# Stationary operands of the expert products widened from 96 to 128 columns

## The reference

```
def clamped_swiglu(h):
    glu, lin = h[..., ::2], h[..., 1::2]
    glu = jnp.minimum(glu, SWIGLU_LIMIT)
    lin = jnp.clip(lin, -SWIGLU_LIMIT, SWIGLU_LIMIT)
    return glu * jax.nn.sigmoid(SWIGLU_ALPHA * glu) * (lin + 1.0)

def expert_block(args):
    tok, gate, e = args
    hid = xt[tok] @ w1[e] + b1[e]          # 1024 -> 2048
    out = clamped_swiglu(hid) @ w2[e] + b2[e]   # 1024 -> 1024
    return out * gate[:, None].astype(out.dtype)
```

## Time and profile before

| | |
|---|---|
| executions, median of three | 1666.47 us (1656.95 to 1667.12) |
| span of the profiled execution | 1658.8 us |
| TensorE busy | 1594.8 us, 96% |
| VectorE busy | 1331.5 us, 80% |
| ScalarE busy | 1027.0 us, 62% |
| GpSimd busy | 609.0 us, 37% |
| HBM read | 443.67 MB |

### The profile page before, as it was taken

How to read it: one execution, slowest core, us unless ns; L and a number is a source line. 1 busy time by engine, 2 the same in 40 slices (tenths; PEclk the granted TensorE clock), 3 DMA queues, 4 the chain that set the end, 5 groups by cost and what they waited for, 6 DMA issues and landing times.

```text
span 1658.8 us, 23226 instructions
## 1 busy us (share of the span) xinstructions
PE 1594.8 (96%) x7860; PEld 1161.0 (70%) x7860; DVE 1331.5 (80%) x1172; ACT 1027.0 (62%) x890; POOL 609.0 (37%) x398
## 2 busy tenths in 40 slices
PE   6999989999998999999999999999999999999993
PEld 5787867897566667777777777777777777777772
DVE  4489755543487999899899899899899899999892
ACT  4534335321366777777777777777777777777772
POOL 5643611331342213434333434333434333434320
PEclk9999989999998999999999999999999999999996
DMA  5322100201569999999999999999999999999984
GB/s 178 123 76 77 15 13 1 103 2 53 191 229 310 370 392 380 368 374 384 377 375 380 372 375 379 381 373 380 369 380 378 379 371 377 378 373 383 381 332 135
DMA packets 146542, 467.08 MB, mean 282 GB/s; under 512 B 21014, under 2 KB 35004, under 8 KB 146428
## 3 DMA queue, kind: packets, MB, share of 16 engines
q1 hardware_dynamic: 136684, 437.36, 70.0%
q0 software_dynamic: 9664, 28.53, 7.3%
q10 hardware_dynamic: 144, 0.52, 0.1%
HBM read 443.67 MB, written 22.71 MB: 281 GB/s over the span
## 4 chain that ended last, share of the span: by engine, by line
PE 86%; DVE 5%; DMA 4%; issue 2%; POOL 1%; ACT 1%; SPq 1%; POOLq 0%; DVEq 0%; ACTq 0%
PE banks L1675 21%; PE banks L1677 20%; PE banks L1676 20%; PE banks L1337 2%; PE banks L1620 2%; PE banks L1338 2%; PE banks L1339 2%; PE banks L1684 2%; PE banks L1526 1%; PE banks L1670 1%; PE banks L1516 1%; PE banks L1403 1%; PE banks L1704 1%; PE banks L1428 1%; DMA x_sum<-xs 1%
## 5 line engine op out<-in xcount | busy, mean ns | idle before, releaser
L2017 DVE TENSOR_TENSOR lo<-slots,hi 128x2048 fp32r<-128x2048 f32 x384 | 862.9, 2287 | 55.0 <-PE banks L1677 48.6
L1126 ACT CAST hi<-slots 128x2048 fp32r<-128x2048 f32 x384 | 733.7, 1911 | 243.7 <-PE banks L1677 124.8
L1675 PE MATMUL banks<-lo,x_hi 128*96 128x512 f32 x1024 | 408.1, 399 | 0.0
L1677 PE MATMUL banks<-hi,x_lo 128*96 128x512 f32 x1024 | 403.4, 394 | 0.0
L1676 PE MATMUL banks<-hi,x_hi 128*96 128x512 f32 x1024 | 402.3, 393 | 0.0
L914 POOL DMA_INDIRECT x_sum<-hT,idy x32 | 91.6, 2862 | 464.5 <-ACT hT L1215 450.0
L939 POOL COPY idx_all<-ovf_pair 96x2 int32 x28 | 162.5, 5803 | 157.4 <-DMA ovf_pair<-slot_tokens,ovf_col 157.4
L1677 PEld LDWEIGHTS banks<-hi,x_lo 128*96 128x96 f32 x1024 | 165.8, 162 | 72.3
L1676 PEld LDWEIGHTS banks<-hi,x_hi 128*96 128x96 f32 x1024 | 166.4, 162 | 67.3
L1675 PEld LDWEIGHTS banks<-lo,x_hi 128*96 128x96 f32 x1024 | 165.9, 162 | 66.6
L1675 PE MATMUL banks<-lo,a_hi 128*96 128x512 f32 x512 | 202.8, 396 | 5.7 <-DVE a_lo L2205 4.1
(11 more groups left out here) (370 smaller groups left out, 1946.9 us busy)
## 6 DMA issues: line engine op xcount, KB each, us to landing
slots<-in_expert_w_dram SPq DMA_DIRECT2D x384, 1024.0 KB, 10.7
slots<-in_w_in_dram SPq DMA_DIRECT2D x13, 1024.0 KB, 5.1
xs<-in_x_dram SPq DMA_DIRECT2D x8, 512.0 KB, 5.9
slots<-in_w_out_dram SPq DMA_DIRECT2D x2, 2048.0 KB, 7.9
x_sum<-xs SPq DMA_DIRECT2D x4, 512.0 KB, 9.4
h_rows<-slots SPq DMA_DIRECT2D x4, 512.0 KB, 3.6
xs<-x_sum SPq DMA_DIRECT2D x4, 512.0 KB, 6.8
x_sum<-xs POOLq DMA_DIRECT2D x3, 512.0 KB, 10.1
```

The lines of the kernel that those rows point to most:

```text
L1126: nc.scalar.copy(w_hi[n % HI][:, :, :], raw[r]).then_inc(hi_ready, 1)
L1675: nc.tensor.matmul(out, x_h, w_l, start=first, stop=False)
L1677: return nc.tensor.matmul(out, x_l, w_h, start=False, stop=last)
L2017: tensor_tensor(w_lo[n % LO][:, :, :], raw[n % RAW], w_hi[n % HI][:, :, :], ALU.subtract).then_inc(lo_ready, 1)
```

## The change

The stationary operands of the expert and bias matmuls become 128 columns wide. The data do not: of x and a the 96 slots of a slice are followed, within the 128 columns, by the first 32 words of what lies behind them in memory, which is the next slice, and behind the last slice 32 words that are cleared once (OVER). x_hi and x_lo become two halves of one tensor, so that behind the last slice of x_hi comes x_lo. The results of those further columns land in partitions 96 to 127 of the PSUM banks, and no one reads them. The selection matrices get 128 columns of the same expert, as two tensors in different regions; the second is therefore filled later, when its region is free.

```
-        x_hi, x_lo = (rounded(f"x_{nm}", "BK", BW, o, [P, KT, NS]) for nm, o in (("hi", 3 * CW), ("lo", 3 * CW + KT * NS)))
-        a_hi = rounded("a_hi", "BK", BW, 3072, [P, FT, NS])
-        sel = rounded("sel", "BK", BW, 3072 + FT * NS, [P, 2, NS])
-        a_lo = rounded("a_lo", "hT", BW, 3 * D, [P, FT, NS])
+        OVER = P - NS
+        x_parts = rounded("x_parts", "BK", BW, 3 * CW, [P, 2 * KT * NS + OVER])
+        a_parts = [rounded("a_hi", "BK", BW, 3 * CW + 2 * KT * NS + OVER, [P, FT * NS + OVER]),
+                   rounded("a_lo", "hT", BW, 3 * D, [P, FT * NS + OVER])]
+        sel = [rounded("sel0", "BK", BW, 3 * CW + 2 * KT * NS + FT * NS + 2 * OVER, [P, P]),
+               rounded("sel1", "hT", BW, 3 * D + FT * NS + OVER, [P, P])]
+        x_hi, x_lo = (x_parts[:, o:o + KT * NS].rearrange("p (k s) -> p k s", s=NS) for o in (0, KT * NS))
+        a_hi, a_lo = (t[:, 0:FT * NS].rearrange("p (k s) -> p k s", s=NS) for t in a_parts)
+
+        def x_columns(part, k):
+            return x_parts[:, (part * KT + k) * NS:(part * KT + k) * NS + P]
+
+        def a_columns(part, f):
+            return a_parts[part][:, f * NS:f * NS + P]
...
-                        nc.tensor.matmul(bank[2 + c][0:NS, :], sel[:, q, :], b1r[:, c * CW:(c + 1) * CW], start=True, stop=False)
+                        nc.tensor.matmul(bank[2 + c], sel[q][:, :], b1r[:, c * CW:(c + 1) * CW], start=True, stop=False)
...
-                        ins = three_products(bank[2 + 2 * half + c][0:NS, :], x_hi[:, k, :], x_lo[:, k, :],
+                        ins = three_products(bank[2 + 2 * half + c], x_columns(0, k), x_columns(1, k),
...
-                        ins = three_products(bank[6 + h][0:NS, :], a_hi[:, f, :], a_lo[:, f, :],
+                        ins = three_products(bank[6 + h], a_columns(0, f), a_columns(1, f),
...
-                nc.vector.tensor_copy(sel[:, q, :].unsqueeze(2), expert_row[:, bass.ds(e, 1)].unsqueeze(1).to_broadcast([P, NS, 1]))\
+                nc.vector.tensor_copy(sel[q][:, :].unsqueeze(2), expert_row[:, bass.ds(e, 1)].unsqueeze(1).to_broadcast([P, P, 1]))\
...
                     if st == ("o", 1, 1):
                         dve.wait_ge(g2_in, 16)
+                        step(nc.vector.memset(x_parts[:, 2 * KT * NS:].bitcast(f32), 0.0))
+                        step(nc.vector.memset(a_parts[0][:, FT * NS:].bitcast(f32), 0.0))
                         set_expert(0, 0)
-                        set_expert(1, 1)
...
             x_low(0, True)
+            step(nc.vector.memset(a_parts[1][:, FT * NS:].bitcast(f32), 0.0))
+            set_expert(1, 1)
             for k in range(1, W1U):
```

## The result

The change made the kernel a little slower. Twenty runs of each kernel give a median of 1665.45 us after (1663.98 to 1673.06) against 1661.76 before (1655.61 to 1667.12), a ratio of 1.0035 with an interval of 1.0023 to 1.0047. That is within 1%, but clearly no gain, and the forecast was 1652 (on the scale of the first three runs of before; 0.9913 of 1661.76 would be 1647). The profiled execution of after has a span of 1663.4 us, against 1658.8.

The account below looks back on a forecast made before the run. TensorE's own matmul stream, 231 ns a step, was taken to pace the expert loop; 29 blocks x 0.48 us (13.9), plus 0.5 and 0.1, made about 14.5 us saved: 1652 on the median's scale, range 1643 to 1668.

Parts of the forecast that it names:

- item 1: Expert-block weight and bias matmuls: 146 steps each 4.2 ns less (230.9 to 226.7), 0.61 us gained per block.
- the paragraph on width: Compared input projection (128 columns, 226.7 ns) with expert loop (4.3 ns more) and put the difference down to width.
- (a): Last w2 product, 96 columns with DMA nearly idle, still takes 230.9 ns a step, so traffic is not what costs.
- (b): Input projection's short product with 8 stationary columns takes 231.1 ns a step, so narrow is slow there too.
- The first rival: Width isn't it: expert-loop step stays at 230.9 ns, 1.6 us lost, 1668 on the median's scale; chance 0.23.
- Items 2 and 3: After each of two transpose groups per block: nine unsettled steps give back 0.08 us, the uncovered first load 0.05.
- Loads: Stationary loads take 191 ns at 128 columns instead of 162 at 96, hidden behind the running matmul.
- Items 5 to 8: Extra PSUM rows free; selection row at most 0.07 us, covered; clears and moved row 0 to 0.4 us once; other engines unchanged.
- The supply: Expert-loop weight transfers must rise from 377 to 382 GB/s; 391 was seen, so no bound, but a close one.
- the milder form of that rival: Expert-loop transfers limited to 380 GB/s: only 8 us gained, 1658; chance 0.11 for supply limiting part or all.
- The rival "slower": Wider expert-stream matmuls never settle and take 235 ns a step, costing 19 us, 1685; chance 0.06.
- The fast load: 128-column loads fall from 191 to about 96 ns, 5.5 us more gained, 1646; chance 0.02.

Follow-up runs that it names:

- pad128: The changed kernel with every 128-column stationary slice in its own 512 bytes, all starting at byte 128; 1652.26 us against 1662.4 before, ratio 0.9935.
- micro: Separate program, no layer computed: 20 streams of 96 matmuls varying stationary width, start and stride; 128 columns took 226.7 ns a step at byte 128, 232.4 at 0.
- micro2: Separate program of 29 more such streams with other starts, widths, 256 moving columns and bf16; 128 columns with both operands at 64 took 226.8 ns, 127 at 128 233.4.

## Why the prediction was wrong

**The step that failed is item 1, and with it the paragraph on width.** "4.2 ns less" in each of 146 steps was read off two streams that differed in width and in place, and was put down to the width. As measured: at the change's places the mean step went from 230.9 to 231.8, 0.9 ns more. At the place of the input projection the same width does give it (pad128: 226.7 settled, block 35.03). The prediction had asked "width or place?" and answered it with (a) and (b), but by place it meant what else was going on at that time (traffic, neighbours). The 8-column product of the earlier trace rows is narrow and also has its slices 32 bytes apart, so it could not decide it; only a stream with the same width at another place can, and in the trace of before there is none. The first rival did hold the fact that decided it: the new operands start 384 bytes apart, not 512. It stood there as a remark with no price, in the case that had 0.23. That rival, step unchanged, gave +1.6 us; the measured +5.6 has 146 x 0.9 ns = 0.13 us a block beside it.

**Items 2 and 3, right.** In pad128 the stream takes nine steps behind each group of transposes to settle, of 231.1 ns in the mean, as put; in the streams of micro that settle it takes between none and nine. In after there is no steady step to come back to, so item 2 had nothing to act on. The first step behind the transposes is 316 ns in after and some 290 before, 0.026 us twice a block, 0.05 as put. Together with the 0.13 of the steps that is 0.18 of the 0.19 us that a block lost.

**Loads, right.** They take 188 to 190 ns and stay hidden. The Trainium skill's page "TensorE: Matmul & The Clock Gate" ("LDWEIGHTS (loading the stationary operand)") divides the columns by 1.2 GHz, which makes an estimate of 27 ns for 32 more; here it is 190 - 162 = 28, while the whole load, 190 ns, is longer than the rule gives. One row of after:

```profile
L1687 PEld LDWEIGHTS banks<-hi,x_parts 128*128 128x128 f32 x1024 | 194.2, 190 | 41.6
```

**Items 5 to 8, right.** No wait speaks of the wider PSUM rows. A selection row takes VectorE 211 to 227 ns instead of 195 to 204, less than the 0.07 us more of item 6. TensorE's first bias matmul of the expert part waits for the selection row that was moved. The same matmul before and after, with the idle time ahead of it in brackets:

```profile
477.32 1.14 PE L1684 MATMUL banks<-b1r,sel 128*96 128x512 f32 x2 [2.18 <-DVE x_lo L2200]
```

```profile
478.27 1.19 PE L1695 MATMUL banks<-b1r,sel 128*128 128x512 f32 x2 [2.28 <-DVE sel L2031]
```

Before, it waited 2.18 us for x_lo, behind which the clear and the row now stand; so the move cost 0.10 us once, within the 0 to 0.4 of item 7. The first three blocks together took 107.9 us, 1.9 less than before (109.8); over the profiles of the kernels here they take 105.7 to 112.1, so nothing is read from that difference.

**The supply, right as a close bound.** In after it wasn't asked. In pad128 382 GB/s were forecast as needed, 381 flowed, and 1.4 to 4 us of the gain were lost, where the milder form of that rival took 6.5 of 14.5.

**The sum.** With the right places the working would have held: 14.5 us forecast, 14.6 by the blocks of pad128, 11.2 to 11.7 in the time. (The 0.46% by which the profiled execution was put below the median compares a span with a time, which is 1.7 us longer in the later runs; the forecast was scaled by the ratio, so this moves nothing.)

**The rival "slower"** asked for steps of 235 that never settle. 231.8 was enough, as its own threshold of 231 said. Its counter-argument, "96-row operands aren't full either", was wrong: 96 rows and 128 columns at the good place take 226.7 ns. **The fast load** didn't come on, as the loads of 190 ns in after show. The bf16 streams of micro2 do show a load that is faster with exactly 128 columns: 98 ns, against 123 with 96.

**Open.** Why the distance modulo 256 counts, why only with exactly 128 columns it yields 226.7, why 96 columns have their best place 64 bytes on, and why 256 moving columns show nothing of it. The runs give the numbers and no mechanism. At a distance of 128 three streams gave 232.2 to 232.4 and two 233.3, so the rule isn't complete.

## What to carry to other kernels

Where fp32r matmuls with 512 moving columns follow each other with a new stationary operand each, lay the stationary slices 512 bytes apart and start them where the moving slices start modulo 256; with 128 columns that is worth 4 to 7 ns of 230.5 to 233.3 a step, and packing slices tightly can cost more than the width brings. With 96 columns the best of the places tried was 64 bytes further (228.3 against 230.8 packed). When two rows of a trace differ in time, list everything that differs between them, addresses too, before one of the differences gets the price. If the trace holds no row that tells two of them apart, give the remark its own chance and price.

## What the runs showed of the hardware

- A stream of fp32r matmuls with 512 moving columns and a new load each costs 226.7 to 234.3 ns a step at the full clock of 2.4 GHz, depending on width and place; in bf16 it is 215.8 in the five streams tried, with 128 and 96 columns at different places. First and last of 47 steps, bf16 with 128 columns at 0:

```profile
553.34 0.38 PE L202 MATMUL banks<-m_bf,s_bf 128*128 128x512 bf16 x1
...
563.48 0.38 PE L204 MATMUL banks<-m_bf,s_bf 128*128 128x512 bf16 x1
```

- For fp32r, 127 columns are slower (233.3 ns) than 128 (226.7), 112 (228.9) and 96 (230.0) at the same place.
- A load of 128 fp32r columns takes 189 ns in the mean of micro2, 127 columns 187, 120 columns 181, 96 columns 161. In bf16 128 columns take 98 ns and 96 columns 123. Every one of them is shorter than its step.
- Executions of one program differ by 7 to 12 us with a mean granted clock of 0.977 to 0.989. Setting the runs against that clock took the scatter down to 1.3 us and made changes of 0.2% readable.
